# Hybrid decoder trunk on one Trainium2 core: the weight stream through ten slots in one order, tile loops written out, folds four tiles apart

## What is computed

```python
def retrieve(xb):
    q = (xb @ w_query).reshape(-1, PEER_HEADS, 2, PEER_QHALF)
    s = jnp.einsum('thpd,pkd->thpk', q, sub_keys)
    sv, si = lax.top_k(s, PEER_TOPK)
    ...
    top_s, top_p = lax.top_k(cand, PEER_TOPK)
    eidx = jnp.take_along_axis(cidx, top_p, axis=-1)
    g = jax.nn.softmax(top_s, axis=-1)
    u = u_tab[eidx]
    act = jax.nn.gelu(jnp.einsum('thkd,td->thk', u, xb))
    w = g * act
    return jnp.einsum('thk,thkd->td', w, v_tab[eidx])
```

## Time and profile before

| what | value |
|---|---|
| median of 3 runs | 1716.95 us (1714.12 to 1721.23) |
| the profiled execution | 1719.39 us |
| its span, first to last instruction | 1717.6 us |
| granted TensorE clock, mean | 0.992 of full speed |
| instructions in the trace | 33,684 |
| read from memory | 531.92 MB |

### The profile page before, as it was taken

How to read it: one execution, slowest core, us unless ns; L and a number is a source line. 1 busy time by engine, 2 the same in 40 slices (tenths; PEclk the granted TensorE clock), 3 DMA queues, 4 the chain that set the end, 5 groups by cost and what they waited for, 6 DMA issues and landing times. The chain is left out here.

```text
span 1717.6 us, 33684 instructions
## 1 busy us (share of the span) xinstructions
PE 1641.6 (96%) x12244; PEld 1526.3 (89%) x12244; DVE 1090.1 (63%) x2433; ACT 212.8 (12%) x617; POOL 485.5 (28%) x423
## 2 busy tenths in 40 slices
PE   9999999899999999999899999999999999999997
PEld 7687899898999999888788888988899999989997
DVE  3362379984699997455546415999359999844442
ACT  2251221111110000000004312111111100000000
POOL 0000001363244446333410001133334444533320
PEclk9999999999999999999899999999999999999999
DMA  4213478999999999999973436799999999999984
GB/s 146 98 62 127 137 267 284 353 373 360 348 408 399 385 398 409 409 410 410 409 273 133 144 127 220 256 355 352 384 353 361 400 391 397 396 402 393 409 340 156
DMA packets 149911, 533.85 MB, mean 311 GB/s; under 512 B 17617, under 2 KB 20434, under 8 KB 149842
## 3 DMA queue, kind: packets, MB, share of 16 engines
q1 hardware_dynamic: 89938, 314.90, 49.0%
q0 software_dynamic: 59904, 218.13, 32.8%
HBM read 531.92 MB, written 1.05 MB: 310 GB/s over the span
## 5 line engine op out<-in xcount | busy, mean ns | idle before, releaser
L236 PE MATMUL ps<-big,raw 128*128 128x160 f32 (+2 forms) x5232 | 844.7, 321 | 25.0 <-DMA raw<-in_u 23.7
L236 PEld LDWEIGHTS ps<-big,raw 128*128 128x128 f32 x5232 | 776.4, 190 | 78.7 <-issue 21.2
L1095 PE MATMUL ps<-big,raw 128*128 (+1 forms) x4096 | 599.6, 303 | 22.4 <-DMA raw<-in_v_rows 7.9
L1095 PEld LDWEIGHTS ps<-big,raw 128*128 128x128 f32 x4096 | 562.9, 190 | 49.8 <-issue 46.7
L1138 POOL DMA_INDIRECT big<-in_u_rows,big x208 | 254.8, 1225 | 858.3 <-DVE big L1264 410.3
L1281 DVE SCALAR_TENSOR_TENSOR big<-big 128x1024 f32<-128x1024 f32 x201 | 258.0, 1283 | 201.7 <-PE ps L1095 105.6
L1138 POOL DMA_INDIRECT big<-in_v_rows,big x208 | 227.5, 1094 | 311.6 <-DVE big L1281 251.1
L1264 DVE CUSTOM_DVE_ANT_0 big<-big 128x1024 f32<-128x1024 f32 x208 | 243.8, 1218 | 9.9 <-DMA big<-in_u_rows,big 9.9
L1178 ACT ACTIVATE big<-ps 128x160 f32 x256 | 77.9, 304 | 547.9 <-PE ps L236 522.4
L1212 DVE MAX8 big<-big 128x8 f32<-128x128 f32 (+1 forms) x99 | 33.6, 339 | 103.5 <-ACT big L1147 91.1
L321 ACT ACTIVATE big<-h 128x272 f32<-128x272 f32 (+1 forms) x32 | 12.6, 419 | 622.9 <-DVE h L1355 572.6
(11 more groups left out here) (165 smaller groups left out, 723.3 us busy)
## 6 DMA issues: line engine op xcount, KB each, us to landing
raw<-in_u SPq DMA_DIRECT2D x256, 512.0 KB
raw<-in_v_rows SPq DMA_DIRECT2D x256, 512.0 KB
raw<-in_query SPq DMA_DIRECT2D x32, 512.0 KB, 3.3
raw<-in_lru_w SPq DMA_DIRECT2D x24, 512.0 KB, 3.4
raw<-in_mla_down SPq DMA_DIRECT2D x17, 512.0 KB, 3.3
raw<-in_mla_out SPq DMA_DIRECT2D x8, 512.0 KB, 3.6
big<-in_u_rows,big POOLq DMA_INDIRECT x208
big<-in_v_rows,big POOLq DMA_INDIRECT x208
```

What stands on the lines that cost most here:

```text
L236: mm = pe.matmul(out, self.mem.raw[:, s, c * P:(c + 1) * P], x[:, c, :], start=(c == 0), stop=(c == DC - 1))
L1095: return pe.matmul(accumulator(c), mem.raw[:, s, c * P:(c + 1) * P], act_w[:, i, :], start=start, stop=False, skip_group_check=True)
```

## The change

`raw` gets ten slots, for which `big` is made smaller by as much (the sum of both is unchanged). All weight tiles of the program form one list in the order of their use, and tile g goes to slot g modulo 10. One `done` semaphore counts through the whole program, and there is one `landed` for each slot. SyncE's part of a stage issues the loads for the tiles that are ten places ahead of that stage's, so that the first ten of the next stage come with it. The loops over tiles are written out on SyncE, ScalarE and TensorE. The folds stand before v tiles 112, 116, 120 (layer 0 only) and 124. A core of the diff, with the parts left out that follow the same pattern:

```diff
-UNROLL = 4
+SLOTS = 10
...
-BIG = NK * L
+BIG = NK * max(L - GATHERED[0], SEQ - GATHERED[1]) + 8 * D
...
-        self.raw = sb("raw", [P, UNROLL, D])
+        self.raw = sb("raw", [P, SLOTS, D])
...
+class Tiles:
+    def __init__(self, ctx, mem, tiles):
+        self.mem, self.tiles = mem, tiles
+        self.landed = [ctx.sem(f"landed{k}") for k in range(SLOTS)]
+        self.done = ctx.sem("tiles_done")
+
+    def fetch(self, sp, first, last):
+
+        for g in range(first, min(last, len(self.tiles))):
+            if g >= SLOTS:
+                sp.wait_ge(self.done, 2 * (g - SLOTS + 1))
+            sp.dma_start(self.mem.raw[:, g % SLOTS, :], self.tiles[g]).then_inc(self.landed[g % SLOTS], 16)
...
-    def multiply_raw(self, pe, turn, s, out, x, scaled=None):
-
-        pe.wait_ge(self.landed[s], turn * 16 + 16)
-        pe.wait_ge(self.free[s % 2], turn * 2 + (s // 2 + 1))
+    def wait_landed(self, pe, n):
+        g = self.base + n
+        pe.wait_ge(self.mem.tiles.landed[g % SLOTS], 16 * (g // SLOTS + 1))
...
+    def multiply_raw(self, pe, n, out, x, scaled=None):
+
+        self.wait_landed(pe, n)
+        pe.wait_ge(self.free[n % 2], n // 2 + 1)
...
 # peer, SyncE
-            st.loaded_before(sp, 1 if layer == 0 else 3)
             sp.dma_start(keys, d["keys"][layer]).then_inc(keys_in, 16)
             sp.dma_start(ident, d["idm"][:, 0:P]).then_inc(keys_in, 16)
-            with sp.Fori(1, TQ) as turn:
-                for s in range(UNROLL):
-                    st.load_read(sp, turn, s, tile_of(d["query"][layer], turn, s))
...
+            mem.tiles.fetch(sp, st.base + SLOTS, st.base + PEER_TILES + SLOTS)
...
 # peer, TensorE
-            v_turn(V0, 0, fresh=True)
-            with pe.Fori(V0 + 1, V0 + NG // 2) as turn:
-                v_turn(turn, (turn - V0) * 2)
-            with pe.Fori(V0 + NG // 2, V1) as turn:
-                v_turn(turn)
-            pe.wait_ge(gated, 2 * NG)
-            with pe.Fori(V1, END - 4) as turn:
-                v_turn(turn)
-
-            folds = {END - 4: range(0, COPIES - 1), END - 1: [COPIES - 1]}
-            for turn in range(END - 4, END):
-                for b in folds.get(turn, ()):
+            fold_before = {NK - 16 + 4 * b: b for b in range(COPIES - 1)}
+            fold_before[NK - 4] = COPIES - 1
+            for i in range(NK - 2):
+                if i == HALF:
+                    pe.wait_ge(gated, 2 * NG)
+                if i in fold_before:
+                    b = fold_before[i]
                     pe.wait_ge(rows_taken, ROWS + min(2 * TOPK * (b + 1), ROWS))
...
+                apply_v(pe, i)
+                if i % 2 and i < 2 * NG:
+                    products(pe, 1, i // 2)
...
+            pe.wait_ge(chunk_done, DC)
+            pe.sem_inc(st.done, 4)
```

More of the change, by code:

```diff
@@ L188, in keep_busy, with __init__ @@
         pe.matmul(mem.ps[:, bank, 0:2 * P], mem.filler[:, 0:P], mem.filler[:, :], start=True, stop=True)
-class Stream:
[L198 to L212, removed]
-        for s in range(UNROLL):
[L215 to L222, removed]
+class Tiles:
[8 more added lines that the diff above has]
+            sp.dma_start(self.mem.raw[:, g % SLOTS, :], self.tiles[g]).then_inc(self.landed[g % SLOTS], 16)
+class Stream:
+    def __init__(self, ctx, mem, name, base, tokens):
+        self.mem, self.base, self.T = mem, base, tokens
+        self.done = mem.tiles.done
+        self.free = [ctx.sem(f"{name}_free{r}") for r in range(2)]
     def open(self, pe):
@@ L432, in _ @@
             sp.dma_start(posi[0:1, META:L], d["pos"]).then_inc(pos_in, 16)
[L433 to L448, removed]
+            mem.tiles.fetch(sp, 0, MLA_TILES + SLOTS)
         @block.gpsimd
@@ L728, in update_residual @@
     next_sum.gather(dve, DC - 1)
-def tile_of(tiles, turn, s):
-    return tiles[bass.ds(turn * UNROLL + s, 1)].rearrange("a p f -> p (a f)")
 def rglru(nc, ctx, mem, d):
@@ L776, in _ @@
         def _(sp):
-            st.loaded_before(sp, 2)
             sp.dma_start(wa, d["lru_wa"]).then_inc(w_in, 16)
             sp.dma_start(wx, d["lru_wx"]).then_inc(w_in, 16)
-            with sp.Fori(1, END) as turn:
-                for s in range(UNROLL):
-                    st.load_read(sp, turn, s, tile_of(d["lru_w"], turn, s))
-            st.read_ahead(sp, END, d["query"][1])
+            mem.tiles.fetch(sp, st.base + SLOTS, st.base + LRU_TILES + SLOTS)
         @block.scalar
@@ L916, in _ @@
                               stop=True).then_inc(gated, 1)
-            for s in range(UNROLL):
-                st.multiply_raw(pe, OUT, s, st.bank(s), b, states if s == 0 else None)
-            with pe.Fori(OUT + 1, END) as turn:
-                for s in range(UNROLL):
-                    st.multiply_raw(pe, turn, s, st.bank(s), b)
+            for n in range(OUT, OUT + DC):
+                st.multiply_raw(pe, n, st.bank(n), b, states if n == OUT else None)
             keep_busy(pe, mem, 6, 14)
@@ L1344, in _ @@
                 tile = NG * 2 + k * (LAST_ROW_TILE - NG * 2) // left
-                dve.wait_ge(st.done, V0 * HALVES + 2 * tile)
+                st.wait_halves(dve, 2 * (QUERIES + NK + tile))
                 n = rows(n, n + 1)
@@ L1398, in _, with u_product @@
                 score(GG + g, [qt[:, half, g, :, :].rearrange("p h t -> p (h t)") for half in range(2)])
-            def u_product(turn, s):
-                st.multiply_raw(pe, turn, s, mem.ps[:, s % 2, 0:TD], xn[:, :, 0:TD])
-            def u_tiles(first, last):
-                with pe.Fori(first, last) as turn:
-                    for s in range(UNROLL):
-                        u_product(turn, s)
-            u_tiles(U0, SPREAD)
+            def u_product(i):
+                st.multiply_raw(pe, QUERIES + i, mem.ps[:, i % 2, 0:TD], xn[:, :, 0:TD])
+            for i in range(SPREAD):
+                u_product(i)
             pe.wait_ge(placed, SPREADS)
@@ L1497, in trunk @@
         with Stage(nc) as whole:
-            mem.ahead = [whole.sem(f"ahead{s}") for s in range(UNROLL)]
+            mem.tiles = Tiles(whole, mem, tiles_in_order(d))
             with Stage(nc) as own:
```

182 lines of the change are left out of this document (79 added, 103 removed).

## The result

The changed kernel took 1672.05 us (median of 4 runs, 1671.31 to 1673.24), beside 1719.09 us before (4 runs, 1714.12 to 1724.45): a ratio of 0.9726, 95% interval 0.9694 to 0.9759. The forecast was 1663 with a range of 1642 to 1698.

A forecast was written before the change was run, and what follows sets the result against it. TensorE's pace and the DMA's were taken as two close limits. Layer 0's -23 and layer 1's -32 us took 1719.4 to 1664.4; about half of a 2.4 us profile excess off gave 1663, range 1642 to 1698.

The forecast's parts named there:

- What bounds it: Whole kernel: TensorE at 2.175 us a tile and the DMA at 2.56 us per tile and row lie close together.
- Ten slots, layer 0: Layer 0 up to v tile 124: ten slots recover most of 29 us of unsaturated DMA time, -23 us, bounds -33 and 0.
- I leave 10 of the 29: Layer 0's last row: 10 of 29 us stay lost to bursts, moments with both stocks full, and half the code traffic.
- Ten slots, layer 1: Layer 1: TensorE is the limit and nine tenths of its 35.9 us loss goes, -32 us, bounds -36 and -17.
- the 20 us it had to spare by the count: Layer 1 at v tile 118: DMA could be done at 1625 us, TensorE without its loss at 1645.5.
- Folds four tiles apart: Folds before the last v tiles: moves TensorE's wait, not the DMA's end; 0 beyond the sum, bounds 0 and -5.9 us.
- Loops written out: Tile loops on SyncE, ScalarE and TensorE: worth 0, same TensorE pace in and out of a loop; 68 more code packets.
- the 7 us for packets in layer 0's ten: Layer 0: 7 us allowed for fetching added code, within the 10 us left unrecovered; none put into layer 1.
- A: Rival: TensorE's new code packets all use one DMA engine and delay tiles; 1688 us, chance 0.18.
- C: Rival: TensorE runs out of instructions at each new packet of straight code; 88 us added, 1751 us, chance 0.08.
- VectorE's points: Before softmax and spread products: VectorE's idle 17.5 and 10.6 us (layer 0), 24.7 and 8.1 (layer 1) shorten as TensorE comes earlier.
- First loads: Program start: ten tiles issued in place of four, behind the inputs in the same queue; 0, at most 2 us either way.

## Why the prediction was right, and where its terms were off

In spans the change gave 48.1 us of the 55 forecast. Without the 3.0 that are chance at the start it would be 45, still well inside the range, so that the range holds is not luck, while the nearness of single terms partly is.

**What bounds it.** Confirmed. The time lost before was the DMA idling while TensorE waited, and depth alone brings it back; the DMA's 2.56 us for a tile and a row holds with ten slots as with four (46 tiles in 117.5 us). The Trainium skill ("DMA: Bandwidth & Descriptors", Queues, rings and completion order) says that a DMA engine takes the queues that have work in turn, a packet at a time. By that rule a deeper queue gets no larger share of the turns; the trace agrees: beside those 46 tiles the stream's queue has 6584 packets and the gathers' 6585.

**Ten slots, layer 0: -23 forecast, -17.6 measured, of which 4.2 stand before the layer's first u tile.** The mechanism is as forecast, and the size of one term was off: "I leave 10 of the 29". Against the second profile of the kernel before it is 10.3, so the shortfall may be larger than it looks. Counted from a start 4.2 us earlier, the last row should have been added by 855.1; it was by 862.8, 7.7 later. Stretches of the kernel after, with VectorE's rows (L1230):

```profile
271.90:407.00 135.10, 0.00 (x0) 1.00 0.99 383
407.00:421.50 14.50, 0.00 (x0) 1.00 1.03 409
421.50:624.90 203.40, 18.21 (x15) 1.00 1.03 408
624.90:802.80 177.90, 89.67 (x70) 1.00 1.03 409
802.80:833.40 30.60, 14.13 (x11) 1.00 1.03 409
833.40:850.00 16.60, 8.55 (x7) 0.65 1.03 410
850.00:862.80 12.80, 8.15 (x7) 0.50 0.51 205
```

The u stretch loses (410 - 383) / 410 x 135.1 = 8.9 us, the others at 408 and 409 some 1.5. That is the size of the 10 that I left, but partly by luck: 7 of them stood for packets, of whose delay ten slots show nothing, and most of what the trace shows is a DMA that still idles in the u stretch. The last line was in no term: the DMA is half idle, which is (410 - 205) / 410 x 12.8 = 6.4 us. The six tiles of the next stage that find a free slot are in by then, the transfers thin out, and the last three rows are then added one behind the other:

```profile
858.68 4.12 DVE L1230 SCALAR_TENSOR_TENSOR big<-big 128x1024 f32<-128x1024 f32 x3 [0.75 <-DMA big<-in_v_rows,big]
```

The sum let the last row follow the last unit at full rate, with 1.28 us for one addition. Another 1.7 are the fold at the low clock, 3.4 for the 1.7 of the forecast: I priced it by a fold with no wait before it, and it now stands behind one of 27 us. The earlier trace rows had the right price: the third fold there, behind a wait of 5.9, takes 3.4 us until the next tile, at a granted clock of 0.50.

**Ten slots, layer 1: -32 forecast, -30.5 measured** (-35.8 against the second profile, so that it comes this close is in part chance). TensorE is the limit in the u stretch as forecast (15.9 us of it). The late v stretch gave 9.5 of its 16.6: its stock is empty from about tile 79, and the DMA's pace rules the last tiles, in spite of the 20 us it had to spare by the count. It took 163.7 us, where the forecast wanted it within 160. The rest came from outside these two stretches, 2.5 us of it from the six u tiles behind the spread products, a piece that took 15.7 and takes 13.2.

**Folds four tiles apart: 0 forecast, about +4 to +5 with ten slots.** This is the step that was wrong in kind. "Alone this moves TensorE's wait, not the DMA's end" overlooked that a waiting TensorE holds slots, and full slots keep the stream off the rows. The prediction's own count had "up to 6 of the next stage's" tiles before the last row; it did not ask what a different place of the fold would do to them. With four slots the two versions are at ratios 1.0053 and 1.003, whose intervals overlap, so there the cost isn't shown.

**Loops written out: 0, with the 7 us for packets in layer 0's ten.** With four slots they cost about 5 us in the whole program. With ten, six packets fall into 683 to 800.5 and the 46 tiles take 2.55 us each all the same. TensorE is at the DMA's pace there, so no landed tiles are left that could cover a packet. What differs is how the queues share the DMA, which moves 409 GB/s in both: with four slots (690.27 to 795.00) the gathers' queue got 5973 packets and the stream's 5763, with ten (694.4 to 796.6) 5730 and 5726. So with four slots the stream loses turns to the rows; that more loads in the queue are what prevents it fits, but no run isolates it. A's way of going wrong is real, a tile held up by a packet, but it costs 0.45 us a packet, and only with few slots. A packet was under way for 1.05 us on average, where the forecast had 0.9. C did not happen: TensorE was idle for want of instructions ("issue") for 0.6 us over all u tiles, with four slots and the folds back for 3.4. The Trainium skill ("Runtime: NRT & Kernel Launch", Instruction fetch mechanics) calls the cost of crossing a block mostly hidden. For TensorE's supply of instructions the trace agrees, with these 0.6 us; but with four slots a packet's transfer delayed the data, 0.45 us each.

**VectorE's points.** As forecast TensorE pulled them along. The wait before softmax was 17.5 us in layer 0 and 24.7 in layer 1; it is gone in layer 0 and 8.5 in layer 1. Before the spread products 18.7 us of waiting became 7.4, all of it in layer 1.

**First loads.** 0 forecast; 1.2 of the 4.2 us at the start lie beyond what two executions of the kernel before differ by, inside the 2 that were allowed.

Where it stays open: which DMA engines a packet occupies, why ten slots are spared its delay, and how firm the parts of a few us are, since each was read off one execution and two of the same kernel differ by 4 us in layer 0.

## What to carry to other kernels

Where a stream and bursts share the DMA, compare GB/s in the stretches where the consumer waits with those where both queues are backed up: the difference bounds what a deeper buffer can bring back (here 31.6 us of unsaturated time in layer 0, of which 13.4 came back). A deep prefetch takes what it is given: at a stage's end it loads the next stage before the last rows of this one, unless something holds it, so put the consumer of the rows last and the stream behind them. And ask of each wait which buffers it keeps occupied: an early wait with full slots gave the late rows the whole DMA.

## What the runs showed that I had not expected

- A wait instruction whose semaphore has long been reached took 48 ns of TensorE's time between passes (32 a tile made 2.175 us into 3.70), and one such instruction can hold two of the program's waits.
- A 16 KB code packet delayed a 512 KB tile by about 0.45 us with the DMA full and four slots; with ten slots no delay showed.
- After 27.1 us without passes the granted clock was 0.50 of full speed (1.2 GHz; it had fallen by 840 and stayed there), and a fold of 16 passes took 3.4 us for 1.8. Behind a wait of 11.4 us and a fold, a v tile took 4.3 us for 2.175.
